# A product-key expert layer on one core: four gathered token tiles, keys in two passes, values in one

## The chip, the core and the metric

The kernel runs on one core of one Trainium2 chip. Its engines work at the same time, each on its own list of instructions, and meet at semaphores: TensorE (PE) multiplies, VectorE (DVE) does elementwise work and top-k, ScalarE (ACT) activations and copies, GpSimd (POOL) here elementwise work and indirect transfers, SyncE (SP) queues the plain transfers. The metric is the device time of one execution in microseconds (us); the figure quoted for a kernel is the median of its runs.

## The reference

One encoder layer over 1024 tokens of width 1024, all in float32. First a mixer (normalise, project, gated linear attention and pooling, project back), which the change does not touch. Then the expert part:

```python
q = (ht @ w_q).reshape(T, 8, 2, 128)                        # 8 retrieval heads, 2 halves
s = einsum('thpd,hpnd->thpn', q, sub_keys)                  # 128 scores per half
vals, idx = top_k(s, 16)                                    # per half
cand = vals[:, :, 0, :, None] + vals[:, :, 1, None, :]      # 16 x 16 sums
top_s, top_pos = top_k(cand.reshape(T, 8, 256), 16)
i1, i2 = the two indices that top_pos picks from idx
experts = i1 * 128 + i2                                     # 128 chosen of 16384 experts per token
gates = softmax(top_s)
a = gelu(h . u[experts]);  y = sum_e gates * a * v[experts]
out = x + gate2 * rmsnorm(y)
```

## The kernel before

Tokens lie in 8 tiles of 128. The 16384 experts lie in 128 blocks of 128. Every float32 product is made of three passes over split operands: an operand is cut into a high and a low part (ACT writes `hi` as a copy in the reduced type, `split_hi`, L78; DVE writes `lo` as the difference, `split_lo`, L83), and PE adds hi·hi, hi·lo and lo·hi (`tile_product`, L93).

**Retrieval** (`retrieval_scores`, L1093). For each of 16 half-heads PE makes a query tile (`tile_product`, 48 matmuls of 512 columns) and then the scores of all 8 token tiles (L1196). In each turn DVE splits both of the next weights first, then takes both scores out of PSUM, and then runs `topk_head` (L1028) for token tile 0 of that head. All scores go to memory (`s_d`), and later each head of a tile comes back as `s_work`.

**Sweep 1** (`expert_sweep_1`, L1264). For each of the 128 expert blocks PE computes the keys' products with all 1024 tokens (48 matmuls of 512 columns), ACT applies gelu (L1415), and the result is stored (`act_d`). Beside it, one head of one token tile after another gets its top-k on DVE. For the first 6 tiles (`DENSE`) the sparse gates become dense matrices: for groups of 8 tokens DVE compares the iota row with the chosen indices in two instructions of 1024 elements (`compare`, L1479), POOL multiplies by the gate in two (L1393), PE makes 8 matmuls of 256 columns (L1555), ACT copies the high part out (L1426) and DVE adds the low part (L1492). The last 2 tiles (`SPARSE`) keep their lists of chosen experts. The order on each engine is written out by hand: a step is two expert blocks, and PE runs product, gates, product, gates, so that a batch of one-hots is compared while PE is in the product before the one after which they are used.

**Sweep 2** (`expert_sweep_2`, L1594). The 6 dense tiles are taken in two rounds of 3, and each round reads all 128 blocks of v. A step is one block: DVE makes the coefficients gate times activation (L1763) and the low parts, ACT the high parts, PE 18 matmuls of 512 columns (L1882) into 3 accumulators. Beside it the 2 sparse tiles are gathered: POOL issues for each of 256 chosen experts an indirect transfer of one activation per token (`pick_acts`, L1666) and one of the v row per token (`fetch_row`, L1674, 512 KB), and DVE adds coefficient times row (`add_row`, L1785). At the end each tile is normalised, scaled and added to x1.

## Time and profile before

| | us |
|---|---|
| runs (3) | 3317.35, 3335.14, 3335.84; median 3335.14 |
| profiled execution, first to last instruction (span) | 3333.3 |
| PE, DVE, ACT, POOL busy in the span | 3133.5, 2255.8, 1016.9, 1005.3 |
| first key matmul of sweep 1 starts | 719.5 |
| first value matmul of sweep 2 starts | 2225.9 |
| last value matmul starts | 3307.1 |
| mean granted clock of PE, whole span | 0.976 |

The page of the profile gives the busy time of each engine; matmuls are pipelined, so their own durations overlap, and what one costs is read from the distance between starts. The span is one execution; what lies around it is the difference to the time of a run, 1.8 us against the median. A timeline merges equal instructions that follow each other and gives their count.

### The profile page before, as it was taken

What the parts mean: (1) busy time and instruction counts of PE and PEld (TensorE: products, weight loads), DVE (VectorE), ACT (ScalarE), POOL (GpSimd) and SP (SyncE); (2) the same over time, 40 slices, a digit from 0 to 9 for tenths busy, and PEclk for the clock granted to TensorE, in tenths of its full rate; (3) what the DMA queues carried; (4) which work ended last, traced back from release to release, by engine and by line L of the source; (5) the groups of instructions that cost most, each with busy time, mean ns of one, the idle gap of its engine ahead of it and who ended that gap; (6) DMA issues with size and microseconds to landing.
All of it is one profiled execution on the core that took longest, in us unless ns stands there. A gap on an engine that the chain in (4) does not pass through costs nothing. (4 is left out here: it accounts for less than half of the span.)

```text
span 3333.3 us, 44756 instructions
## 1 busy us (share of the span) xinstructions
PE 3133.5 (94%) x14706; PEld 2592.3 (78%) x14706; DVE 2255.8 (68%) x3986; ACT 1016.9 (31%) x1301; POOL 1005.3 (30%) x735
## 2 busy tenths in 40 slices
PE   3993799989999999999999999998999998999996
PEld 3881587878888888888888888876888886788885
DVE  6345643567767677675876754436888888888886
ACT  3123442112232232322222221122333334333333
POOL 0000100013222233232332310024555567765541
PEclk9995899999999999999999999999999999999998
DMA  6510122222333324333233332248999999999995
GB/s 235 189 50 8 49 105 93 84 72 113 126 148 139 148 88 151 141 149 137 101 142 145 150 137 106 102 159 299 373 353 361 364 357 332 369 357 364 348 361 186
DMA packets 251520, 640.90 MB, mean 192 GB/s; under 512 B 28864, under 2 KB 134464, under 8 KB 249792
## 3 DMA queue, kind: packets, MB, share of 16 engines
q1 hardware_dynamic: 204528, 498.87, 40.8%
q0 software_dynamic: 46928, 141.20, 11.3%
q8 instruction: 37, 0.61, 0.1%
q14 instruction: 27, 0.22, 0.0%
HBM read 505.76 MB, written 134.22 MB: 192 GB/s over the span
## 5 line engine op out<-in xcount | busy, mean ns | idle before, releaser
L1393 POOL TENSOR_TENSOR onehot<-onehot,slots 128x1024 fp32r<-128x1024 f32 x192 | 368.9, 1943 | 1180.1 <-DVE onehot L1479 1180.1
L93 PE MATMUL acc_u<-a_hi,u_hi 128*128 128x512 f32 x2048 | 633.1, 391 | 2.5 <-PEq L1114 2.5
L93 PE MATMUL acc_u<-a_lo,u_hi 128*128 128x512 f32 x2048 | 632.3, 390 | 0.0
L93 PE MATMUL acc_u<-a_hi,u_lo 128*128 128x512 f32 x2048 | 631.6, 389 | 0.0
L1882 PE MATMUL y_ps<-v_hi,c_hi 128*128 128x512 f32 x1536 | 477.2, 392 | 32.6 <-DVE c_lo L83 26.8
L1882 PE MATMUL y_ps<-v_lo,c_hi 128*128 128x512 f32 x1536 | 475.8, 391 | 0.0
L1882 PE MATMUL y_ps<-v_hi,c_lo 128*128 128x512 f32 x1536 | 474.6, 390 | 0.0
L78 ACT ACTIVATE v_hi<-v_raw 128x1024 fp32r<-128x1024 f32 x256 | 271.6, 1061 | 654.0 <-PE y_ps L1882 544.8
L93 PEld LDWEIGHTS acc_u<-a_lo,u_hi 128*128 128x128 f32 x2048 | 385.0, 188 | 81.0
L93 PEld LDWEIGHTS acc_u<-a_hi,u_lo 128*128 128x128 f32 x2048 | 384.8, 188 | 81.2
L83 DVE TENSOR_TENSOR v_lo<-v_raw,v_hi 128x1024 fp32r<-128x1024 f32 x256 | 316.6, 1237 | 186.4 <-ACT v_hi L78 145.1
L1415 ACT ACTIVATE gelu<-acc_u 128x1024 f32<-128x1024 f32 x128 | 131.5, 1028 | 1013.8 <-PE acc_u L93 1013.8
L93 PEld LDWEIGHTS acc_u<-a_hi,u_hi 128*128 128x128 f32 x2048 | 378.4, 188 | 75.0 <-issue 2.6
L1674 POOL DMA_INDIRECT v_rows<-in_v,eidx x256 | 283.5, 1107 | 358.0 <-DVE y_part L1785 313.4
L1882 PEld LDWEIGHTS y_ps<-v_hi,c_hi 128*128 128x128 f32 x1536 | 288.3, 189 | 99.1 <-DVE v_lo L83 26.0
L1882 PEld LDWEIGHTS y_ps<-v_lo,c_hi 128*128 128x128 f32 x1536 | 289.9, 189 | 60.9
L1882 PEld LDWEIGHTS y_ps<-v_hi,c_lo 128*128 128x128 f32 x1536 | 289.7, 189 | 60.9
L1666 POOL DMA_INDIRECT picked_act<-act_d,aidx x256 | 311.1, 1215 | 77.9 <-issue 77.9
L1785 DVE SCALAR_TENSOR_TENSOR y_part<-v_rows,coef,y_part 128x1024 f32<-128x1024 f32 x256 | 329.2, 1289 | 0.6 <-DMA v_rows<-in_v,eidx 0.5
L83 DVE TENSOR_TENSOR u_lo<-u_raw,u_hi 128x1024 fp32r<-128x1024 f32 x128 | 164.8, 1288 | 207.5 <-ACT u_hi L78 207.5
L1492 DVE TENSOR_TENSOR gate_block<-gate_block,gate_ps 128x1024 f32 (+1 forms) x96 | 116.8, 1216 | 216.0 <-ACT gate_block L1426 216.0
L1479 DVE TENSOR_TENSOR onehot<-consts,slots 128x1024 fp32r<-128x1024 f32 x192 | 239.6, 1290 | 0.9 <-issue 0.9
(228 smaller groups left out, 3414.4 us busy)
## 6 DMA issues: line engine op xcount, KB each, us to landing
v_raw<-in_v SPq DMA_DIRECT2D x256, 512.0 KB
u_raw<-in_u SPq DMA_DIRECT2D x128, 512.0 KB, 4.3
act_d<-gelu SPq DMA_DIRECT2D x128, 512.0 KB, 2.6
gate_d<-gate_block SPq DMA_DIRECT2D x12, 4096.0 KB, 12.1
gt<-gate_d SPq DMA_DIRECT2D x64, 768.0 KB
at<-act_d SPq DMA_DIRECT2D x256, 192.0 KB
w_mod_b<-in_w_mod SPq DMA_DIRECT2D x6, 2560.0 KB, 9.1
w_mod<-in_w_mod SPq DMA_DIRECT2D x9, 1024.0 KB, 16.4
```

Of the source, the lines that this page charges most:

```text
L78: return act.activation(hi, raw, ACT.Copy)
L83: return dve.tensor_tensor(lo, raw, hi.bitcast(F32), ALU.subtract)
L93: done = pe.matmul(acc[:, cols], w, a[:, k, cols], start=first, stop=last)
L1393: last_op = pool.tensor_tensor(onehot_2[u][:, :, part, :], onehot_2[u][:, :, 0, :].bitcast(F32), gate.unsqueeze(2).to_broadcast([P, TOK // ...
L1415: act.activation(gelu[s][:], acc[s][:], ACT.Gelu).then_inc(gelu_done, 1)
L1479: last = dve.tensor_tensor(rows, g.iota.unsqueeze(1).to_broadcast([P, TOK // 2, NKEYS]), chosen.unsqueeze(2).to_broadcast([P, TOK // 2, NK ...
L1492: dve.tensor_tensor(dst, dst, gate_psum(1), ALU.add).then_inc(gate_out, 1)
L1666: pool.indirect_dma_start(out=picked_act[:, e:e + 1], out_offset=None, in_=act_table, in_offset=bass.IndirectOffsetOnAxis(ap=index(g.aidx, ...
L1674: pool.indirect_dma_start(out=rows[e % UNROLL][:], out_offset=None, in_=v_table, in_offset=bass.IndirectOffsetOnAxis(ap=index(g.eidx, e), ...
L1785: dve.scalar_tensor_tensor(sums, rows[k][:], coef[:, k:k + 1], sums, ALU.mult, ALU.add).then_inc(rows_done, 1)
L1882: done = pe.matmul(yps[t][:, cols], c, v[s][:, cols], start=first and k == 0, stop=last and k == 2)
```

## The change

It rewrites everything behind the mixer as one block with every loop written out (no loop instructions). Four token tiles are gathered instead of two and four are dense instead of six. The keys are read twice: steps m = 0 to 127 give the activations of token tiles 0 to 2 (`EARLY`, 384 columns), steps 128 to 255 those of tiles 3 to 7 (`LATE`, two pieces of 320 columns). The values are read once, in steps 256 to 383, for the four dense tiles. The candidate list of a head is cut from 256 to 136 sums (the first row's 16, and 8 of each of the other 15). Top-k of the three early tiles is done together in retrieval, a head at a time; the other five tiles are done in pairs of heads, one or two of 13 stages per step, from step 5 on. The dense gates are made from step 44 on in one batch of 8 tokens every third step, by three short instructions for each token on DVE; POOL has no elementwise work left. The 512 gathered rows begin at step 134, with two in a step, and three in steps 200 to 255. Gate blocks are stored for 16 tokens at a time, and read back in pieces of 512 bytes in place of 1 KB. Rings: 4 raw blocks, 3 split blocks, 7 gathered rows.

```diff
+EARLY = 3
+GATHERED = 4
+LATE = TT - EARLY
+DENSE = TT - GATHERED
 DTOK = DENSE * P
-TILE_STEPS = HEADS + 1
-STEPS = NKEYS // 2
-assert DENSE * TILE_STEPS + HEADS + 2 == STEPS
+HEAD_TILES = EARLY
+STAGES = 4
+RAWS, SPLITS, GELUS, ACTS, ROWS = 4, 3, 3, 4, 7
...
+HEADS_STAGES = ((0, 1, 2), (3, 4, 5), (6, 7, 8, 9), (10, 11, 12))
+STEP_STAGES = ((0, 1), (2,), (3,), (4, 5), (6, 7), (8, 9), (10,), (11,), (12,))
+TOPK_FROM, TOPK_PERIOD = 5, 40
+BATCH = 8
+GTOK = 2 * BATCH
+GROUP = 8
+GATES_FROM, GATES_EVERY = 44, 3
+ROWS_FROM, ROWS_FAST = 134, 200
...
-def topk_head(g, dve, h, topk_done):
...
+def topk_stage(g, dve, stage, scores, tops_out, chosen_out, read_all, done):
...
+    dve.drain()
+    if stage == 0:
+        for c in cs:
+            for p in range(2):
+                dve.max(vals[:, c, p, 0:8], scores[c][p])
+    elif stage == 1:
+        for c in cs:
+            for p in range(2):
+                dve.max_index(idx[:, c, p, 1 - p:9 - p], vals[:, c, p, 0:8], scores[c][p])
+                last = dve.match_replace(rest[:, c, p, :], vals[:, c, p, 0:8], scores[c][p], LOWEST)
...
+    elif stage == 2:
+        for c in cs:
+            for p in range(2):
+                dve.max(vals[:, c, p, 8:16], rest[:, c, p, :])
...
+    elif stage == 3:
+        for c in cs:
+            for p in range(2):
+                dve.max_index(idx[:, c, p, 9 - p:17 - p], vals[:, c, p, 8:16], rest[:, c, p, :])
+        dve.tensor_tensor(cand[:, 0:n, 0:TOPK], vals[:, 0:n, 0, 0:1].to_broadcast([P, n, TOPK]), vals[:, 0:n, 1, :], ALU.add)
+        later = [P, n, TOPK - 1, TOPK // 2]
+        dve.tensor_tensor(cand[:, 0:n, TOPK:].rearrange("p c (a b) -> p c a b", b=TOPK // 2),
+                          vals[:, 0:n, 0, 1:].unsqueeze(3).to_broadcast(later),
+                          vals[:, 0:n, 1, 0:TOPK // 2].unsqueeze(2).to_broadcast(later), ALU.add)
+    elif stage == 4:
+        for c in cs:
+            dve.max(tops[:, c, 0:8], cand[:, c, :])
+    elif stage == 5:
+        for c in cs:
+            dve.max_index(pos[:, c, 0:8], tops[:, c, 0:8], cand[:, c, :])
+            dve.match_replace(spare[:, c, :], tops[:, c, 0:8], cand[:, c, :], LOWEST)
+    elif stage == 6:
+        for c in cs:
+            dve.max(tops[:, c, 8:16], spare[:, c, :])
+    elif stage == 7:
+        for c in cs:
+            dve.max_index(pos[:, c, 8:16], tops[:, c, 8:16], spare[:, c, :])
+        dve.tensor_copy(tops_out, tops[:, 0:n, :])
+    elif stage == 8:
+        dve.tensor_scalar(hilo[:, 0:n, :, 0], pos[:, 0:n, :], 3, None, ALU.logical_shift_right)
+        dve.tensor_scalar(hilo[:, 0:n, :, 1], pos[:, 0:n, :], float(TOPK), 8.0, ALU.is_lt, ALU.mult)
+    elif stage == 9:
+        dve.scalar_tensor_tensor(hilo[:, 0:n, :, 1], hilo[:, 0:n, :, 1], 7, pos[:, 0:n, :], ALU.bitwise_or, ALU.bitwise_and)
+    elif stage == 10:
+        full = [P, n * TOPK * 2, TOPK + 1]
+        dve.tensor_tensor(match, hilo[:, 0:n].rearrange("p c k l -> p (c k l)").unsqueeze(2).to_broadcast(full),
+                          g.iota[:, 0:TOPK + 1].unsqueeze(1).to_broadcast(full), ALU.is_equal)
+    elif stage == 11:
+        full = [P, n, TOPK, 2 * (TOPK + 1)]
+        each = match.rearrange("p (c k l) i -> p c k (l i)", k=TOPK, l=2)
+        dve.tensor_tensor(each, each, idx[:, 0:n].rearrange("p c l i -> p c (l i)").unsqueeze(2).to_broadcast(full), ALU.mult)
+    else:
+        dve.tensor_reduce(chosen_out, match, AX, ALU.add).then_inc(done, 1)
+def rows_by(m):
+    if m < ROWS_FROM:
+        return 0
+    return min(GATHERED * CHOSEN, 2 * (m - ROWS_FROM + 1) + max(0, min(m, 2 * N - 1) - ROWS_FAST + 1))
+def split_expert_hi(g, act, m):
+    act.wait_ge(g.raw_in[m % RAWS], 16 * (m // RAWS + 1))
+    if m >= SPLITS:
+        act.wait_ge(g.tile_done, m - SPLITS + 1)
+    split_hi(act, g.hi[m % SPLITS][:], g.raw[m % RAWS][:]).then_inc(g.hi_ready, 1)
+def expert_product(g, pe, m):
+    pe.wait_ge(g.lo_ready, m + 1)
+    if m >= 2:
+        pe.wait_ge(g.gelu_done, m - 1)
+    else:
+        pe.wait_ge(g.q_out, QTILES - 1 + m)
+    acc, w_hi, w_lo = g.mps[m % 2], g.hi[m % SPLITS], g.lo[m % SPLITS]
+    if m < N:
+        parts = [(acc[:, 0:EARLY * P], slice(0, EARLY * P))]
+    else:
+        wide = LATE * P // 2
+        parts = [(acc[:, half * HALF:half * HALF + wide], slice(EARLY * P + half * wide, EARLY * P + (half + 1) * wide))
+                 for half in range(2)]
+    for k in range(KC):
+        wh, wl = w_hi[:, k * P:(k + 1) * P], w_lo[:, k * P:(k + 1) * P]
+        for w, a, first, last in ((wh, g.a_hi, k == 0, False), (wh, g.a_lo, False, False), (wl, g.a_hi, False, k == KC - 1)):
+            for dst, cols in parts:
+                done = pe.matmul(dst, w, a[:, k, cols], start=first, stop=last)
+    done.then_inc(g.tile_done, 1)
+def retrieval_scalar(g, act):
+    def stage_out(n):
+        act.wait_ge(g.s_done, n + 1)
+        if n >= STAGES:
+            act.wait_ge(g.s_stored[n % STAGES], 16 * (n // STAGES))
+            act.wait_ge(g.heads_read, (n - STAGES) // 2 + 1)
+        act.activation(g.stage[n % STAGES][:], g.sps[n % 2], ACT.Copy).then_inc(g.s_out, 1)
+    for n in range(QTILES):
+        act.wait_ge(g.q_done, n + 1)
+        act.activation(g.q[n % 2][:], g.mps[n % 2][:], ACT.Copy).then_inc(g.q_out, 1)
+        if n + 2 < QTILES:
+            act.wait_ge(g.wq_in[n % 2], 16 * (n // 2 + 2))
+            split_hi(act, g.wq_hi[n % 2][:], g.wq_raw[n % 2][:]).then_inc(g.wq_hi_ready, 1)
+        else:
+            split_expert_hi(g, act, n + 2 - QTILES)
+        if n:
+            stage_out(n - 1)
+    stage_out(QTILES - 1)
+def retrieval_vector(g, dve):
+    def split(n):
+        dve.wait_ge(g.wq_hi_ready, n + 1)
+        split_lo(dve, g.wq_lo[n % 2][:], g.wq_raw[n % 2][:], g.wq_hi[n % 2][:]).then_inc(g.wq_lo_ready, 1)
...
+    for h in range(HEADS - 1):
+        split(2 * h + 2)
+        dve.wait_ge(g.s_out, 2 * h + 2)
+        for stage in range(5):
+            head_stage(g, dve, h, stage)
+        split(2 * h + 3)
+        for stage in range(5, TOPK_STAGES):
...
+            head_stage(g, dve, h, stage)
+    split_expert_lo(g, dve, 1)
+    dve.wait_ge(g.s_out, QTILES)
+def retrieval_tensor(g, pe):
+    def product(n, halves=(0, 1)):
+        pe.wait_ge(g.wq_lo_ready, n + 1)
+        tile_product(pe, g.mps[n % 2], g.wq_hi[n % 2], g.wq_lo[n % 2], g.a_hi, g.a_lo, halves).then_inc(g.q_done, 1)
+    def score(n):
+        pe.wait_ge(g.q_out, n + 1)
+        if n >= 2:
+            pe.wait_ge(g.s_out, n - 1)
+        for t in range(TT):
+            last = pe.matmul(g.sps[n % 2][:, t, :], g.q[n % 2][:, t * P:(t + 1) * P], g.keys[:, n, :], start=True, stop=True)
+        last.then_inc(g.s_done, 1)
+    for n in range(2):
+        product(n, halves=(1,))
...
+    for n in range(2, QTILES):
+        score(n - 2)
+        product(n)
+    score(QTILES - 2)
+    expert_product(g, pe, 0)
+    score(QTILES - 1)
+def sweeps_scalar(g, act):
...
+    for m in range(3 * N):
+        if m >= 2 * N - 1 and m + 1 < 3 * N:
+            split_coefficients(m + 1 - 2 * N)
+        if m + 2 < 3 * N:
+            split_expert_hi(g, act, m + 2)
+        x, batch = gate_turn(m - 1)
+        if x is not None and batch >= 0:
+            gate_evacuation(x * GATE_BATCHES + batch)
...
+        if m < 2 * N:
+            activate(m)
...
+def sweeps_vector(g, dve):
...
+    def onehots(b, u):
...
+        for t in range(BATCH):
+            col = slice(first + t, first + t + 1)
+            high = g.gate_hi[:, col].bitcast(F32)
+            dve.tensor_scalar(g.onehot_1[u][:, t, :], g.iota, g.slots[:, 0, col], None, ALU.is_equal)
+            dve.tensor_scalar(g.onehot_2[u][:, t, 0:NKEYS], g.iota, g.slots[:, 1, col], high, ALU.is_equal, ALU.mult)
+            last = dve.tensor_scalar(g.onehot_2[u][:, t, NKEYS:], g.iota, g.slots[:, 1, col], g.slots[:, 2, col],
+                                     ALU.is_equal, ALU.mult)
+        last.then_inc(g.onehot_ready, 1)
...
+    for m in range(3 * N):
+        if 2 * N - 2 <= m < 3 * N - 2:
+            coefficients(m + 2 - 2 * N)
+        if m + 2 < 3 * N:
+            split_expert_lo(g, dve, m + 2)
+        if 2 * N - 1 <= m < 3 * N - 1:
+            coefficients_lo(m + 1 - 2 * N)
+        first_tiles(m)
+        x, batch = gate_turn(m - 1)
+        if x is not None and batch < 0:
+            take_slots(x)
+        elif x is not None:
+            add_gate_low(x * GATE_BATCHES + batch)
+        topk_steps(m)
+        x, batch = gate_turn(m)
+        if x is not None and batch >= 0:
+            onehots(x * GATE_BATCHES + batch, m // N)
...
+        for e in range(rows_by(m - 1), rows_by(m)):
+            add_row(e)
+            if e % CHOSEN == CHOSEN - 1:
+                sum_gathered(e // CHOSEN)
...
+def sweeps_gpsimd(g, pool):
...
+    turns = GATHERED * CHOSEN // TURN
+    pool.wait_ge(g.chosen_ready, 1)
+    act_complete(N - 1)
+    for s in range(2):
...
+    pick_acts(0)
+    for turn in range(turns):
+        for e in range(turn * TURN, (turn + 1) * TURN):
+            fetch_row(e)
+            if e == turn * TURN and turn + 1 < turns:
+                pick_acts(turn + 1)
+def sweeps_tensor(g, pe):
...
+    def dense_product(n):
+        m = 2 * N + n
+        pe.wait_ge(g.lo_ready, m + 1)
+        pe.wait_ge(g.clo_ready, n + 1)
...
+        for q, t in enumerate(DENSE_ORDER):
...
+            ch, cl = g.c_hi[s][:, t * P:(t + 1) * P], g.c_lo[s][:, t * P:(t + 1) * P]
+            for k, (c, v) in enumerate(((ch, v_hi), (ch, v_lo), (cl, v_hi))):
+                for half in range(2):
+                    cols = slice(half * HALF, (half + 1) * HALF)
+                    done = pe.matmul(g.yps[t][:, cols], c, v[:, cols], start=n == 0 and k == 0, stop=n == N - 1 and k == 2)
+            if n == N - 1:
+                done.then_inc(g.y_summed, 1)
+        if n < N - 1:
+            done.then_inc(g.tile_done, 1)
+    for m in range(2 * N):
+        if m:
+            expert_product(g, pe, m)
+        x, batch = gate_turn(m)
+        if x is not None and batch < 0:
+            transpose_slots(x)
+        elif x is not None:
+            gates(x * GATE_BATCHES + batch, m // N)
+    for n in range(N):
+        dense_product(n)
```

## Rows read from the trace of the kernel before

**Rows 1.** The page, part 1: busy time of each engine, share, instructions.
```profile
PE 3133.5 (94%) x14706; PEld 2592.3 (78%) x14706; DVE 2255.8 (68%) x3986; ACT 1016.9 (31%) x1301; POOL 1005.3 (30%) x735
```
**Rows 2.** Tile views: count, ns min/median/max, first and last start, forms.
```profile
L93 PE MATMUL acc_u<-a_hi,u_hi x2048: 387/389/628, 719.5 to 2217.5; 128*128 128x512 f32 x187
...
L1882 PE MATMUL y_ps<-v_hi,c_lo x1536: 387/389/628, 2227.8 to 3307.1; 128*128 128x512 f32 x192
```
**Rows 3.** Sweep 2: length, busy (count) by engine, clock, DMA share, GB/s.
```profile
2500.00:2600.00 100.00, 100.00 (x443) 82.81 (x442) 83.35 (x102) 36.48 (x50) 56.20 (x51) 1.00 0.98 363
```
**Rows 4.** The chain that ended last: start, length, instruction, count.
```profile
2275.98 488.45 PE y_ps L1882 x2142
```
**Rows 5.** Timeline, sweep 1: start, length, engine, instruction, count [idle before].
```profile
1200.26 1.11 PE L1555 MATMUL gate_ps<-onehot,onehot 128*128 128x256 f32 x8
1200.45 1.03 ACT L1415 ACTIVATE gelu<-acc_u 128x1024 f32<-128x1024 f32 x1 [8.84 <-PE acc_u L93]
1201.21 0.63 PE L93 MATMUL acc_u<-a_hi,u_hi 128*128 128x512 f32 x2
```
**Rows 6.** Timeline of PE in retrieval, around one query tile.
```profile
700.66 1.95 PE L1196 MATMUL s_ps<-keys,q 128*128 x16
...
713.35 3.73 PE L1196 MATMUL s_ps<-keys,q 128*128 128x128 f32 x32
```
**Rows 7.** Timeline of DVE: one head's top-k in sweep 1.
```profile
1207.19 0.48 DVE L1032 MAX8 vals<-s_work 128x8 f32<-128x128 f32 x2
1207.75 0.09 DVE L1035 MATCH_VALUE_LOAD idx<-vals,s_work 128x8 f32 x1
...
1208.28 0.08 DVE L1035 MATCH_VALUE_LOAD idx<-vals,s_work 128x8 f32 x1
...
1210.06 1.43 DVE L1043 TENSOR_TENSOR cand<-vals 128x256 f32<-128x256 f32 x1
...
1214.17 0.17 DVE L1058 TENSOR_SCALAR hilo<-pos 128x16 uint32<-128x16 uint32 x1
1214.25 0.17 DVE L1059 TENSOR_SCALAR hilo<-pos 128x16 uint32<-128x16 uint32 x1
1214.49 0.69 DVE L1062 TENSOR_TENSOR match<-hilo,consts 128x512 f32<-128x512 uint32 x1
```
**Rows 8.** Timeline of DVE: after that head, and early in sweep 1.
```profile
756.29 4.05 DVE L1479 TENSOR_TENSOR onehot<-consts,slots 128x1024 fp32r<-128x1024 f32 x2
...
1216.71 1.21 DVE L1492 TENSOR_TENSOR gate_block<-gate_block,gate_ps 128x1024 f32 x1
1217.84 1.22 DVE L83 TENSOR_TENSOR u_lo<-u_raw,u_hi 128x1024 fp32r<-128x1024 f32 x1
1218.97 2.36 DVE L1479 TENSOR_TENSOR onehot<-consts,slots 128x1024 fp32r<-128x1024 f32 x2
```
**Rows 9.** Groups of DVE instructions: count, busy us, mean ns, idle before.
```profile
L1785 DVE SCALAR_TENSOR_TENSOR y_part<-v_rows,coef,y_part 128x1024 f32<-128x1024 f32 x256 | 329.2, 1289 | 0.6 <-DMA v_rows<-in_v,eidx 0.5
...
L257 DVE TENSOR_SCALAR x<-x,rstd 128x1024 f32<-128x1024 f32 x8 | 5.4, 746 | 0.1
...
L1258 DVE TENSOR_SCALAR aidx<-eidx,token_col 128x128 uint32<-128x128 uint32 x2 | 0.6, 288 | 0.2
```
**Rows 10.** A stretch early in sweep 1, columns as in rows 3.
```profile
740.00:764.00 24.00, 17.60 (x74) 14.66 (x73) 22.96 (x54) 6.13 (x6) 13.34 (x7) 0.79 0.21 71
```
**Rows 11.** Timeline of PE in that stretch: gate matmuls after a wait.
```profile
749.85 2.08 PE L1555 MATMUL gate_ps<-onehot,onehot 128*128 128x256 f32 x8 [6.40 <-DVE gate_block L1492]
```
**Rows 12.** Timeline of POOL in sweep 2: indirect transfers, issued without waiting.
```profile
2504.78 1.67 POOL L1666 DMA_INDIRECT picked_act<-act_d,aidx  x1 [0.30 <-issue]
...
2516.68 0.94 POOL L1674 DMA_INDIRECT v_rows<-in_v,eidx  x1 [0.30 <-issue]
...
2549.32 0.94 POOL L1674 DMA_INDIRECT v_rows<-in_v,eidx  x1 [0.30 <-issue]
...
2553.41 0.93 POOL L1674 DMA_INDIRECT v_rows<-in_v,eidx  x1 [0.30 <-issue]
```

1212 lines of the change are left out of this document (473 added, 739 removed).

## The prediction, before the result was known

> **What bounds the kernel now.** The page's first part says PE is busy 94% of the span [rows 1], so I read PE first: the tile views give the ends of the stages, sweep 1 from 719.5 and the last value matmul at 3307.1 [rows 2], that is 2587.6 us for both sweeps and 26 us behind them. Next the distance between starts. A run of 2142 matmuls of 512 columns takes 488.45 us, 0.228 each [rows 4]; 8 matmuls of 256 columns take 1201.21 - 1200.26 = 0.95, 0.119 each [rows 5]. Between the two I interpolate 0.146 for 320 columns and 0.1735 for 384. The old work at these prices is 128 x 48 x 0.228 = 1401, plus 96 gate batches x 0.95 = 91, plus 256 x 18 x 0.228 = 1051: 2543 of the 2588. So PE's rate is the bound and all else together costs 45 us. In sweep 2 the transfers are near their own limit, busy 0.98 at 363 GB/s [rows 3]. DVE is busy 68% [rows 1] and hides, since its work stands a step ahead of PE.
>
> **PE's own work after.** An early key step is 24 x 0.1735 = 4.16 us, a late one 48 x 0.146 = 7.01, a dense value step 24 x 0.228 = 5.47. Times 128: 533, 897 and 700. Gates: 64 batches x 0.95 = 61. Sum 2191, which is **-397** against the 2588. The whole gain is here: 1536 fewer value matmuls, paid with only 29 us for the second reading of the keys.
>
> **Retrieval: a new wait.** Before, DVE splits both next weights before it turns to the scores. After, `split(2h+3)` stands behind stages 0 to 4 of head h, and head h begins only when both its scores are out; PE makes score 2h+1 directly ahead of product 2h+3, which needs that split. So from the end of product 2h+2: ACT copies the query, splits, copies the scores, 3 x 1.03 = 3.1 [rows 5]; then DVE's stages for 3 tiles. MAX8 costs 0.24, an index search with its replacement 1208.28 - 1207.75 = 0.53 [rows 7], half of that for a search alone. 6 x 0.24 + 6 x 0.53 + (6 x 0.24 + 0.1) + (6 x 0.26 + candidates 1.8) + 3 x 0.25 + 5 drains x 0.07 = 10.6 (candidates: 360 elements at the 1.2 to 1.43 per 256 of [rows 7]). Then the split, 1.13 [rows 8]. Together 14.9, where PE would start after the score, 12.69 [rows 6] - 10.94 = 1.75. That is 13.1 a head, 7 heads: 92. The second half (stages 5 to 12: 9.8 by the same rows, with three instructions of 1632 elements scaled from 0.69 per 512) ends before product 2h+3 does. After such a gap PE also restarts at the half clock: one wait of 6.4 us left 8 gate matmuls at 2.08 instead of 1.11 [rows 5, 11] and a granted clock of 0.79 over 24 us [rows 10]; 74 matmuls in 17.6 busy us where 15.1 would do, 2.5 lost. 7 x 2.5 = 17. **+109**, with cover gone completely: it's in order on PE.
>
> **Gates: DVE can't be ahead of PE.** The high split of block m+2 waits for product m-1 (3 split buffers), DVE begins step m with that block's low split, and then come low-gate addition, top-k, and last the one-hots that PE waits for right behind product m. What is queued behind the wait on PE is product m+1, on ACT the gate copy and the next gelu. From the end of product m-1: gelu of 384 columns 0.4, split 1.03 [rows 5], low split 1.13 [rows 8], a drain 0.07, top-k 1.3 (in the gate steps mostly stages 2, 3, 5 to 9, 11, 12 of two heads), one-hots. These are 24 instructions of 128 elements per batch, a form the trace doesn't show. Nearest: one with a pointer scalar and 128 elements takes 288 ns [rows 9], and followers start about 0.085 before the end of the one ahead (0.17 against 1214.25 - 1214.17 = 0.08 [rows 7]; 1.22 against 1.13 [rows 8]); two thirds of them have a second pointer. I take 0.21, a batch 5.1. Ends: 0.14 (between the 0.08 for 16 elements and 746 ns for 1024 [rows 7, 9]), 3.4 a batch; 0.26 if they run at one element a cycle, 6.3. So the one-hots are there 9.05 us after the end of product m-1 and PE at 4.16: 4.9 a batch. Early: 26 batches, 127. Half-clock restarts: 20 (26 x 2.5 = 65 at most, as the waits are shorter than 6.4; zero at least). The last head's top-k (20 us in steps 0 to 3 beside 4.16 a step, two steps of slack): 6. **+153**.
>
> The VectorE page of the Trainium skill (VectorE: DVE Perf Modes, Mode 2×_2P) says a float32 instruction with a single source in SBUF takes two elements a cycle and one with two sources takes one. The 746 ns for 1024 elements beside 1.22 for a difference [rows 8, 9] agree; by it the upper end falls away.
>
> **Late keys.** Gelu of 640 columns is 0.7, so the one-hots come at 2.95 + 5.1 + top-k 2.0 (1.3 in the fifth tile) against 7.01: 3.0 and 2.3. 22 batches: 58. The 2 rows a step cost DVE 1.2 each [rows 9] and fit. From step 200 to 255 three rows are taken in each step, 168 rows. POOL pays per row one pick, (2516.68 - 2504.78)/8 = 1.49, and one fetch, (2553.41 - 2549.32)/3 = 1.36 [rows 12]: 2.85, so 8.55 a step; ring and DVE are in order, and PE follows two steps later. 56 x 8.55 = 479 against 408 of PE: 71. Lower end 1.24 + 1.24, the shortest with their 0.30 [rows 12]: 9. POOL's issues beside short DVE instructions: a comparison pair took 4.05 early in sweep 1, while POOL multiplied, and 2.36 in [rows 8] without it, so the two engines do hold each other up. For 15 batches I take 2 us each of 5.1: 30, between zero and 77. **+159**.
>
> **Dense values.** A step moves 512 KB of v, 256 of activations, 256 of gates and two rows of 512: 2.10 MB. At 363 GB/s over 0.98 [rows 3] that is 5.66, and the 512-byte pieces are not better; POOL's two rows want 5.7. I take 5.8 in 106 steps: +35 against 5.47 (ends 0 and +67, at 6.1). DVE has 0.6 + 1.13 + 0.6 + 2.4 + 0.1 = 4.85 and fits. Hand-over between the passes: **+40** together. Stores of gates and activations, the x1 loads on SP and the 3.7 us of finishing a gathered tile lie beside PE and I cost them at nothing; they'd show as up to 4 us for each of 4 tiles.
>
> **Tail.** Before, 26 us from the last matmul, with a sparse tile's finish in the way. After, four tiles end 1.4 us apart in PE and DVE needs 2.7 each: 12. **-14**.
>
> Sum: -397 + 109 + 153 + 159 + 40 - 14 = +50, so the profiled 3333.3 becomes 3383; the median lies 2 above its span: **3385 us, slower by 1.5%**.
>
> **Rivals.** (A) *The short one-hots are cheap.* At 0.14 a piece and without half-clock restarts: 48 batches x 1.7 = 82 and 20 less, 3283: faster. For it: 0.08 for a 16-element instruction. Against: 288 ns. It ends on the other side of the old time from 4.1 us a batch down, 3.4 being its end. (B) *POOL and the transfers keep up*: 62 + 30 + 35 less, 3258, faster; for it the shortest issues, against it that every eight picks in [rows 12] average 1.49. (C) *POOL is locked out.* If the DVE's short instructions keep it out for the whole batch, 15 x 5.1 = 77 in place of 30, and with every early wait restarting at the half clock, 45: 3477.
>
> The SBUF page (SBUF — State Buffer, Who interferes with whom) states this as a rule for the Trainium skill's single-source DVE modes: GpSimd can't write its transfer descriptors while such an instruction runs. No run here shows it for transfers. By that rule case C's 47 us would be the price.
>
> (D) *The wait in retrieval isn't there*, because I misread the order: 109 less, 3276.
>
> **Numbers.** Main case 0.50, its own range 3310 to 3460 (one-hots by 0.02 a piece is 23 us, POOL 30, transfers 30, restarts 20). A 0.17, B 0.12, C 0.15, D 0.04, the rest 0.02. The range of 8 in 10 reaches into A and B below and C above: 3240 to 3490; all low ends at once would be 3133, all high ends 3515. A measurement of this kernel can tell about 1% from no change, 3302 to 3368. Faster: over half of A, most of B and D, a little of the main case, 0.26. Within 1%: the rest of A and B and a fifth of the main case, 0.23. Slower 0.51.
>
> **What the changed profile would show.** PE idle some 13 us ahead of each odd query product, released by the DVE split; the first key matmul of step 1 about 110 later. One-hot instructions starting 0.21 apart, PE idle 4.9 before each early gate batch and 2 to 3 before late ones. Key steps from 200 on at 8.5 us, DVE waiting for row transfers. Dense steps at 5.8, transfers busy near 1. It'd be wrong at once if PE is busy over 95% between first key and last value matmul.

## The result: 9.8% slower, outside the range

The changed kernel takes **3658.2 us** (median of 4 runs, 3651.1 to 3669.8), the kernel before 3334.5 beside it (3317.4 to 3335.8): ratio **1.098**, interval 1.095 to 1.101. Forecast were 3385 and at most 3490. The direction was right, the size wrong by 273 us.

The profiled execution spans 3657.6 us. The page's first part, which answers to [rows 1] (engine, busy us, share of the span, instructions), has a PE that is no longer the bound by itself:

```profile
PE 3003.9 (82%) x15980; PEld 2705.5 (74%) x15980; DVE 2400.1 (66%) x5118; ACT 940.1 (26%) x1262; POOL 1313.0 (36%) x1033
```

The tile view of the key and value products (first and last start) gives the ends of the stages, as [rows 2] did:

```profile
L1308 PE MATMUL mix<-a_hi,hi x3072: 302/309/633, 814.2 to 2820.8; 128*128 128x320 f32 x128, 128*128 128x384 f32 x64
...
L1774 PE MATMUL mix<-hi,free_hi_r x680: 387/389/628, 2829.8 to 3645.8; 128*128 128x512 f32 x170
```

Against the prediction's own terms, put together by stage (us; the end of the early key steps, 1583, is the start of the gelu of the last of them):

| stage | predicted | measured | miss |
|---|---|---|---|
| up to the first key product | 828 | 814 | -14 |
| 128 early key steps | 711 | 768 | +57 |
| 128 late key steps | 1092 | 1239 | +147 |
| 128 value steps | 740 | 824 | +84 |
| tail | 12 | 12 | 0 |

Four stretches of it by engine (length, then busy us of PE, its weight loads, DVE, ACT, POOL, granted clock, transfer share, GB/s; compare [rows 3, 10]): early key steps with gates, late ones at two rows a step, late ones at three, value steps:

```profile
1000.00:1584.00 584.00, 438.62 (x2286) 430.31 (x2285) 394.02 (x1252) 159.86 (x208) 0.00 (x0) 0.87 0.41 134
1640.00:2254.00 614.00, 537.64 (x3422) 526.45 (x3421) 470.53 (x1134) 137.82 (x162) 324.00 (x262) 0.94 0.67 227
2254.00:2822.00 568.00, 471.62 (x2818) 448.75 (x2817) 394.52 (x663) 115.62 (x138) 387.91 (x333) 0.87 0.75 262
2845.00:3499.00 654.00, 571.23 (x2350) 462.99 (x2349) 475.88 (x518) 161.55 (x199) 535.88 (x388) 0.94 0.89 318
```

PE is full in none of them, and neither are the transfers. GpSimd is, in the last one: 535.88 us busy and 0.30 between any two of 388 transfers make 652 of the 654 us, though the page counts only the first as busy. What ended PE's idle time (what waited, for what, total us, times, longest):

```profile
PE sps_all L1756 <- DVE onehot L1567: 145.4, 26, 7.5
PE mix L1308 <- issue: 87.0, 120, 2.4
PE mix L107 <- DVE wq_lo L97: 82.2, 8, 11.6
PE sps_all L1756 <- DVE free_hi_r L1567: 73.8, 26, 6.2
PE sps_all L1774 <- DVE free_hi_r L97: 49.4, 12, 5.9
...
PE sps_all L1756 <- issue: 27.6, 15, 5.0
```

The one-hots and the retrieval wait are the two that were forecast. The second line was in no theory: "issue" is time in which PE waited for nothing that the profile shows, 87 us of it in the middle of key products. Sweep 1 before had none. The last line, ahead of gate matmuls, is mostly something else. Its long waits end right behind the last one-hot of their batch, as here (PE, then DVE):

```profile
1750.80 1.44 PE L1756 MATMUL sps_all<-free_hi_r 128*128 128x256 f32 x5 [4.98 <-issue]
```
```profile
1750.41 0.33 DVE L1567 TENSOR_SCALAR free_hi_r<-consts,slots 128x128 fp32r<-128x128 f32 x1
```

So about 24 of the 27.6 us are the forecast wait for one-hots under another name, and some 90 us in all are not explained. They look like this, PE first (start, length, instruction, count, idle before) and then GpSimd at the same time:

```profile
1602.91 0.46 PE L1308 MATMUL mix<-a_lo,hi 128*128 128x320 f32 x2
1603.20 0.65 PE L1308 MATMUL mix<-a_hi,lo 128*128 128x320 f32 x2
1604.25 0.31 PE L1308 MATMUL mix<-a_hi,hi 128*128 128x320 f32 x1 [0.39 <-issue]
1604.97 0.31 PE L1308 MATMUL mix<-a_hi,hi 128*128 128x320 f32 x1 [0.41 <-issue]
1605.68 0.41 PE L1308 MATMUL mix<-a_lo,hi 128*128 128x320 f32 x1 [0.40 <-issue]
1607.08 0.43 PE L1308 MATMUL mix<-a_lo,hi 128*128 128x320 f32 x1 [0.98 <-issue]
1608.47 0.43 PE L1308 MATMUL mix<-a_hi,lo 128*128 128x320 f32 x1 [0.97 <-issue]
```
```profile
1587.19 1.16 POOL L1714 DMA_INDIRECT picked_act<-act_early,aidx  x1 [1172.49 <-DMA act_early<-gelu]
...
1607.72 0.94 POOL L1714 DMA_INDIRECT picked_act<-act_early,aidx  x1 [0.30 <-issue]
1608.97 0.94 POOL L1721 DMA_INDIRECT rows<-in_v,eidx  x1 [0.30 <-issue]
...
1615.19 0.94 POOL L1721 DMA_INDIRECT rows<-in_v,eidx  x1 [0.30 <-issue]
```

Two matmuls together had taken 0.29 from start to start; now each starts by itself, 0.70 or 1.40 after the one ahead. It begins some 16 us after GpSimd started to issue and ends at 1619.7, 3.5 us after GpSimd paused. I call PE **held** here. "Held" times below are the issue waits less those that end right behind a one-hot.

### The profile page after: what moved, and what is told of

The parts are those of the page before. It is cut to its first block, busy times and chain, and to the rows that moved or that the text cites. A ratio compares the mean times of both kernels' runs of the same rounds, so it can differ in the third digit from the quotient of the medians.

```text
span 3657.6 us, 43230 instructions
## 1 busy us (share of the span) xinstructions
PE 3003.9 (82%) x15980; PEld 2705.5 (74%) x15980; DVE 2400.1 (66%) x5118; ACT 940.1 (26%) x1262; POOL 1313.0 (36%) x1033
## 3 DMA queue, kind: packets, MB, share of 16 engines
q0 software_dynamic: 90112, 268.76, 21.0%
q8 instruction: 123, 2.02, 0.2%
## 4 chain that ended last, share of the span: by engine, by line
PE 42%; DVE 15%; POOL 15%; issue 9%; ACT 2%; DMA 1%; DVEq 1%; another core or an unknown queue 0%; SPq 0%; ACTq 0%; POOLq 0%
PE mix L1308 30%; POOL picked_act L1714 8%; POOL rows L1721 7%; PE mix L107 5%; PE sps_all L1756 3%; DVE lo L97 2%; PE sps_all L1774 2%; PE mix L1774 2%; ACT hi L92 2%; DVE free_hi_r L1567 2%; DVE onehot L1567 1%; DVE onehot L1566 1%; DVE free_hi_r L1566 1%; DVE onehot L1565 1%; DVE free_hi_r L1565 1%
## 5 line engine op out<-in xcount | busy, mean ns | idle before, releaser
L1714 POOL DMA_INDIRECT picked_act<-act_early,aidx x384 | 465.6, 1213 | 1289.2 <-DMA act_early<-gelu 1172.5
L1308 PE MATMUL mix<-a_hi,hi 128*128 128x320 f32 (+1 forms) x3072 | 853.3, 332 | 29.5 <-issue 24.4
L1308 PE MATMUL mix<-a_hi,lo 128*128 128x320 f32 (+1 forms) x3072 | 847.7, 330 | 34.2 <-issue 33.8
L1308 PE MATMUL mix<-a_lo,hi 128*128 128x320 f32 (+1 forms) x3072 | 850.2, 330 | 28.9 <-issue 28.8
L97 DVE TENSOR_TENSOR lo<-raw,hi 128x1024 fp32r<-128x1024 f32 x384 | 469.2, 1222 | 572.9 <-ACT hi L92 477.9
L1721 POOL DMA_INDIRECT rows<-in_v,eidx x512 | 643.0, 1256 | 473.8 <-DVE ys L1626 279.2
L1626 DVE SCALAR_TENSOR_TENSOR ys<-rows,coef,ys 128x1024 f32<-128x1024 f32 x504 | 627.6, 1281 | 168.4 <-DMA rows<-in_v,eidx 151.7
L1308 PEld LDWEIGHTS mix<-a_hi,hi 128*128 128x128 f32 x3072 | 568.1, 200 | 40.5 <-issue 35.1
L1308 PEld LDWEIGHTS mix<-a_hi,lo 128*128 128x128 f32 x3072 | 565.6, 198 | 41.8 <-issue 41.8
L1308 PEld LDWEIGHTS mix<-a_lo,hi 128*128 128x128 f32 x3072 | 568.1, 199 | 34.6 <-issue 34.6
```

The lines of the kernel that those rows point to most:

```text
L97: return dve.tensor_tensor(lo, raw, hi.bitcast(F32), ALU.subtract)
L1308: done = pe.matmul(dst, w, a[:, k, cols], start=first, stop=last)
L1626: dve.scalar_tensor_tensor(sums, row, coef, sums, ALU.mult, ALU.add).then_inc(g.rows_done, 1)
L1714: pool.indirect_dma_start(out=g.picked_act[:, e:e + 1], out_offset=None, in_=act_tables[e // (EARLY * CHOSEN)], in_offset=bass.IndirectOff ...
L1721: pool.indirect_dma_start(out=g.rows[e % ROWS][:], out_offset=None, in_=v_table, in_offset=bass.IndirectOffsetOnAxis(ap=index(g.eidx, e), ...
```

## Experiments

All edits are on the changed kernel. Stage times are from each run's own profile, "late" and "value" between the gelus of products 127 and 255 and the last matmul. 

### The waits that were forecast

**gates_next**: gate matmuls one product later.
```
-        gates(x * GATE_BATCHES + batch, m // N)        # x, batch = gate_turn(m)
+        gates(x * GATE_BATCHES + batch, (m - 1) // N)  # x, batch = gate_turn(m - 1)
```
(the copy, the low addition and the store follow with `gate_turn(m - 2)`).

> The gate matmuls of a batch stand one product later on PE (and their copy, low addition and store one step later); the one-hots are made where they were. Theory O (PE idles because the one-hots are always last on DVE): PE has a product of 4.16 or 7.0 us to cover the 5.6 us of one-hots, so the idle time before gate matmuls (145 us early, 74 late) and the half-clock restarts behind it (some 50) go: early key steps 769 to about 600, late ones 1237 to about 1160, total 3658 to 3400-3440. Rival S (the split ring: the low split two steps on only comes behind the one-hots, so the wait merely moves to the next product): less than 60 us gained. Nothing changes in retrieval (814 to the first key product) or in the value stage (824).

3427.2 us, **231 gained**: early 759 to 613, late 1239 to 1154, value unchanged at 824 ("early" is from the gelu of product 0 to that of product 127). Theory O holds, rival S falls. The wait for the one-hots early fell from 145 to 40.

**split_first**: both retrieval splits ahead of the stages of a head.
```
     split(2 * h + 2)
+    split(2 * h + 3)
     dve.wait_ge(g.s_out, 2 * h + 2)
-    for stage in range(5): head_stage(g, dve, h, stage)
-    split(2 * h + 3)
-    for stage in range(5, TOPK_STAGES):
+    for stage in range(TOPK_STAGES):
```

> DVE splits both next query weights of retrieval before it turns to the scores, as in the kernel before; nothing else differs. Theory W (the 82 us in 7 longer waits of PE for that split, with a restart at the half clock behind each, are the whole of what retrieval lost): first key product 90 to 105 us earlier, total 3555 to 3570. Rival V (the work of DVE in a head, 26 us, is then the bound by itself): gain under 50.

3651.6 us, 7 gained: the key stage began 25 earlier, and 20 were given back in the stages behind. W falls. The trace shows why: DVE now makes both splits behind the whole head, and the wait has only moved to the even product. PE, and DVE at the next head:

```profile
647.90 1.22 PE L107 MATMUL mix<-a_hi,wq_hi 128*128 128x512 f32 x2 [9.22 <-DVE wq_lo L97]
```
```profile
646.64 2.35 DVE L97 TENSOR_TENSOR wq_lo<-wq_raw,wq_hi 128x1024 fp32r<-128x1024 f32 x2
664.86 1.26 DVE L1044 MAX8 vals<-stage 128x8 f32<-128x128 f32 x6 [15.87 <-ACT stage L1341]
```

DVE is idle for 16 us in this head (107.6 in 7 such waits), so DVE's load is not the bound (rival V falls too): the head, the split, the product, the score and the next head form a ring.

**next_and_first**: the two together.

> Gate matmuls one product later and both splits of retrieval first, together. If the two lie in different stages and add up: 3427 less the gain of the split alone (90 to 105), 3322 to 3340, level with the kernel before. If something is shared (the key stage begins earlier but waits for a load or the top-k): over 3360.

3357.7 us: 70 less than with gates_next, between the two expectations. Only 29 of it is the earlier first gelu (800 for 829); the late stage took 1118 for 1154 and the value stage 816 for 824. PE was held less (74 us for 129), which the edit wasn't meant to change. So gains of some ten us behind retrieval can't be put down to an edit alone: in split_first the late stage grew by 33.

**next_and_spread**: gates_next, and the splits spread over the head.
```
+    split(2); split(3)
     for h in range(HEADS - 1):
-        split(2 * h + 2)
         ... stages 0 to 4
-        split(2 * h + 3)
+        if h < HEADS - 2: split(2 * h + 4)
         ... stages 5 to 12
+        if h < HEADS - 2: split(2 * h + 5)
```

> Gate matmuls one product later, and in retrieval the split for product 2h+4 stands after stage 4 of head h and the one for 2h+5 behind stage 12 (with both splits first, 25 us came back of 82). Theory R (retrieval is a ring: DVE's head of 24 us, split, product, score, next head, so the place of the split within the head decides): no wait for the query weights' low halves over 2 us, first key product about 95 us earlier than with the kernel as changed, total 3427 - 95 = 3320 to 3345. Rival V (DVE with 24 us of top-k and two splits a head against 25.4 us of PE is itself the bound): half of it, 3370 to 3390.

3305.1 us (7 runs, 3290 to 3325); ratio to before 0.990, interval 0.988 to 0.992. The wait for wq_lo is gone from the list and the first gelu comes at 731 in place of 824 (829 in gates_next), which is when it came in the kernel before. Theory R holds, though the total is 15 below its range: the ring was the whole of retrieval's loss.

### What the gather costs, and by what

**no_gather, rows_only, picks_only**: GpSimd issues nothing, or only the rows, or only the picks. In each, DVE's multiply-adds stay, with constants for what isn't fetched.
```
-    dve.wait_ge(g.rows_in[e % ROWS], ...)               # no_gather, picks_only
-    pool.indirect_dma_start(out=g.rows[e % ROWS][:], ...)   # picks_only
-    pick_acts(turn + 1)                                 # rows_only
-    turns = GATHERED * CHOSEN // TURN
+    turns = 0                                           # no_gather
```

> Leaves out the gather's transfers: GpSimd issues no picks and no rows; DVE does the same 512 multiply-adds from a constant tile, so its work is unchanged. It measures all that the gather's transfers cost. If the excess of the late key stage (1237 us where PE's own work is 897 + 24) is from the gather, by theory P (GpSimd's issuing holds up PE's and ACT's issue) or T (bytes moved): late stage 1030 to 1060, the one-hot waits (74) staying; value stage 824 to 715-740; total 3658 to 3350-3390. Rival D (DVE's load of one-hots, multiply-adds and splits is the bound in the late stage, whatever is gathered): late stage stays above 1180, total above 3550.

> Leaves out the 512 picks of activations (4 bytes a partition, 0.2% of the gather's bytes, half of GpSimd's instructions); the rows are fetched, DVE's work is the same with constant activations. Theory P (what costs is GpSimd issuing back to back): with half the instructions it is idle half the time, the 115 us of issue waits of PE nearly vanish, late stage about 1080 to 1120, value stage about 740, total 3420 to 3470. Theory T (bytes and DMA engines): nothing to speak of changes, total over 3620. Between them (rows and picks cost alike): 3500 to 3560.

> Leaves out the 512 row fetches (all but 0.2% of the gather's bytes); the 512 picks of 4 bytes a partition are issued in their bursts of 8, and DVE's multiply-adds take a constant row. Leaving all of the gather's transfers out gave 3375 us, leaving out the picks alone 3389, the kernel as changed 3658. Theory N (it's the number of instructions that GpSimd issues, which only with picks and rows together exceeds what fits in a step): 3380 to 3420, as with rows alone. Theory K (the kind: a pick, with its 4-byte packets, holds PE and ACT up as such): 3580 to 3650. Additive (a pick costs half a microsecond wherever): 3640.

| kernel | time | late | value | PE held |
|---|---|---|---|---|
| as changed | 3658.2 | 1239 | 824 | 90 |
| no_gather | 3375.0 | 1080 | 697 | none |
| rows_only | 3388.9 | 1083 | 712 | none |
| picks_only | 3396.7 | 1101 | 697 | 5 |

The gather's transfers cost 283 us, 159 in the late key stage and 127 in the value stage; rows alone, with nearly all the bytes, cost 14, picks alone 22. So each kind alone costs little, and both together cost much. For the rows alone every theory had expected more (3420 at least), and no_gather's late stage is 20 above its forecast. The rows' bytes are no bound: with the rows alone the value steps take 5.56 us at more bandwidth than [rows 3] had (500 us of it):

```profile
2700.00:3200.00 500.00, 499.39 (x2203) 413.21 (x2202) 447.15 (x486) 148.93 (x188) 271.62 (x184) 1.00 1.03 385
```

**rows_halved**: no picks, each row in two transfers.
```
+    for c in (0, HALF):
+        pool.indirect_dma_start(out=g.rows[e % ROWS][:, c:c + HALF], in_=v_halves, ...)
```

> Leaves out the picks and fetches each row in two indirect transfers of 512 elements instead of one of 1024 (of another row of v, so the values are not the reference's): the bytes of the rows alone, but again 1024 instructions on GpSimd, none of them a pick. Theory N (number of instructions): 3600 to 3660, PE's issue waits come back (over 60 us). Theory K (the picks' kind): as with rows alone, 3380 to 3420. A middle value of 3480 to 3540 would say that both count.

3636.6 us, late 1240, value 808, PE held for 69. With no pick but again 1024 instructions nearly the whole loss is back: the **number** of GpSimd's instructions decides. How much of it is their queue and how much is PE being held, this doesn't separate.

**even**: one pick behind each row in place of 8 at a time.
```
-            if e == turn * TURN and turn + 1 < turns:
-                pick_acts(turn + 1)
+            if turn + 1 < turns:
+                pick_acts(turn + 1, [e % TURN])
```

> The picks are no longer issued 8 at a time but one behind each row; same transfers, same number, same work. Theory P1 (PE and ACT are held up only when GpSimd issues without a pause for longer than some ten us): at two rows a step the runs are 5 us, so the issue waits go in steps 134 to 199 and the late stage falls by 80 to 150 us; total 3510 to 3580. Theory P2 (each issue costs PE or ACT the same wherever it stands): no change, 3640 to 3670. Theory T (bytes): no change either. Rival R: rows are issued only every 2.5 us, which is late for DVE in the three-row steps and the value stage: slower by 10 to 40.

3639.8 us, 18 gained; P1's 80 to 150 was wrong. By steps it is less simple: steps 134 to 199 took 585 in place of 601 (578 with no gather) and had next to no held time between 1624 and 2251 (under 1 us; 11 us as changed), where GpSimd's runs without a pause have at most 12 instructions (14 as changed). But at three rows GpSimd has more to issue than fits, its runs get as long as 84, and the steps from 200 took 591 in place of 568 (448 with no gather). There was little to gain where the runs could be cut.

### Who holds PE

**unwaited**: the transfers are issued, nobody waits for them.
```
-    dve.wait_ge(g.rows_in[e % ROWS], 16 * (e // ROWS + 1))
+    sums, row = g.ys[e % 2][:], g.gate_rows[:, 0, :]     # and iota for picked_act
-    pool.wait_ge(g.rows_done, e - ROWS + 1)
+    pool.wait_ge(g.rows_in[e % ROWS], 16 * (e // ROWS))
```

> All 1024 indirect transfers are issued as in the kernel as changed, but nobody waits for them: DVE's multiply-adds take a constant row and constant activations, and GpSimd only waits for the landing of the row seven before. So GpSimd issues nearly without a pause from the 128th key product on, for about 1024 x 1.3 to 1.5 = 1300 to 1500 us. Theory F (freeze: when GpSimd has issued for some 15 us without a pause, PE's and ACT's issue is held up, whoever waits for the rows): PE's issue waits well over the 115 us of the kernel as changed, several hundred us in the late key stage, total above 3650. Theory Q (queueing alone: GpSimd brings the rows late and DVE, in order, waits for them with the splits behind): no issue waits, 3375 to 3420, as with no transfers at all.

**4348.7 us**: late 2056, value 697. Theory Q falls. PE in the held state, and ACT's gelu behind it:

```profile
1889.65 0.43 PE L1308 MATMUL mix<-a_hi,hi 128*128 128x320 f32 x1 [2.37 <-issue]
1892.45 0.43 PE L1308 MATMUL mix<-a_hi,hi 128*128 128x320 f32 x1 [2.37 <-issue]
1895.25 0.43 PE L1308 MATMUL mix<-a_lo,hi 128*128 128x320 f32 x1 [2.37 <-issue]
```
```profile
1851.87 0.70 ACT L1503 ACTIVATE gelu<-mix 128x640 f32<-128x640 f32 x1 [132.75 <-issue]
```

One matmul in 2.80 us. A key product in steady state, 48 weight loads and 48 matmuls, takes 134.4 us, and in that time GpSimd issues exactly 96 transfers (112 in 156.8 us where 8 gate matmuls come on top): **one instruction of PE for one transfer of GpSimd**. In the kernel as changed the hold was mostly milder: a matmul and its weight load in 0.70 or 1.40 us, beside one transfer in 1.25. The SBUF page of the Trainium skill (SBUF — State Buffer, Who interferes with whom) says, of the ports into SBUF, that PE and ACT never wait on anyone. PE was held here; that it was at such a port isn't shown.

**keys24, dense48, plain**, all on unwaited: 24 matmuls of 512 columns in a late key product; 48 of 256 in a value step; plain transfers on the same queue.
```
+    parts = [(acc[:, 0:HALF], slice(EARLY * P, EARLY * P + HALF))]   # keys24
-    for half in range(2):       # columns of 512
+    for quarter in range(4):    # columns of 256                     # dense48
-    pool.indirect_dma_start(out=g.rows[e % ROWS][:], ...)
+    pool.dma_start(g.rows[e % ROWS][:], g.i["v"][e % N])             # plain
```

> On the same kernel the late key products take one matmul of 512 columns where they took two of 320 (24 a product; the products of one of five tiles, and which columns, are left out: the activations are not the reference's). Theory I: key steps are no longer held up; late key stage 128 x 5.5 + 24 + the waits for one-hots at a shorter step (4 to 5 us for 38 batches) = 880 to 950, total 3150 to 3250. Theory K: still 2.80 us a matmul while GpSimd issues, 24 of them 67 us a step: late key stage above 1600, total above 3900.

> On the kernel in which nobody waits for the gather (4349 us; key stage held up, value stage 697 us though GpSimd issued 263 transfers in its first 463 us), each value step takes 48 matmuls of 256 columns in place of 24 of 512. Theory I (PE is sensitive where its instructions come as thick as in the key steps, one matmul per 0.12 to 0.15 us): the value stage is held up while GpSimd issues, 2.8 us a matmul, value stage 1100 to 1200, total 4750 to 4850. Theory K (sensitive is something else of the key stage: its tiles, its PSUM banks, the store of the activations, the early table): only the narrower matmuls show, 48 x 0.119 = 5.7 a step, value stage 730 to 750, total 4380 to 4400.

> On the same kernel GpSimd issues 1024 plain transfers of the same shapes (a fixed row of v, a fixed column of the early activations) in place of the indirect ones. Theory S (every transfer that GpSimd prepares holds PE up): key stage held up as before, total above 4000. Theory X (only indirect ones do): 3375 to 3420, as with no transfers.

keys24: 4200.1, late 1906, still held, at 48 transfers a product: one for one again. dense48: 4540 (the profiled run; the other took 4714), value stage 886; next to untouched for 256 us and then held too, from 3900 until GpSimd was done, at 2.80 a matmul. So neither theory is right: thin instruction streams can be held, and the value stage can be. With its 512-column matmuls it was not: as changed, GpSimd's 388 transfers without a pause held PE nowhere in it. plain: 3464.2, late 1080, no issue wait; theory S falls. PE isn't held while the transfers run at 399 GB/s:

```profile
1780.00:1820.00 40.00, 35.15 (x215) 34.89 (x215) 30.48 (x68) 8.14 (x10) 23.16 (x44) 0.88 1.03 399
```

That clears bytes and packets (90112 packets and 268.76 MB on GpSimd's queue, as in unwaited) of holding PE. They aren't free, though: the total is 44 above theory X, since the value stage took 787. DVE waited there 93 us, in 4 waits, for activations to land, and the transfers' share was 1.02 for its first 239 us. GpSimd was also busy less (0.53 us a transfer, with pauses), so the run doesn't prove that unbroken plain issuing is harmless.

**dense_idle, spaced, unwaited_again**: multiply-adds of 32 columns in the value stage; three small memsets ahead of each transfer; unwaited unchanged.

> On the kernel in which nobody waits for the gather (4349 us), DVE's multiply-adds in the value stage are cut from 1024 to 32 columns, so that DVE is idle there for 2 us more in each step; PE's work is as before. Theory R (PE is held up where GpSimd's transfers follow at their shortest distance, 1.25 us; in the value stage DVE's work stretches them to 1.76): GpSimd speeds up to 1.3 to 1.4 a transfer and PE is held in the value stage, value stage 900 to 1050, total 4550 to 4700. Theory E (what PE executes decides, or whether it has to wait): value stage 697, total 4350, whatever GpSimd's distance.

> On the same kernel GpSimd sets a small spare tile to zero three times ahead of each transfer, and waits for each, so that transfers follow about 1.8 to 2.2 us apart, still without an idle moment on GpSimd. Theory R: PE isn't held up, late key stage 1080 to 1130, total under 3450 (GpSimd's 1024 transfers may outlast the value stage, and then the end is later by that). Theory E or F (GpSimd's being busy all the time decides): one PE instruction per transfer as before, now 2 us each: late key stage over 2100.

> The same kernel as unwaited (4349 us in two rounds), run again in another session. If being held up goes with the kernel (its instruction streams and their exact timing), all rounds are again held: 4330 to 4370, late key stage 2050. If it goes with the session or the chip, it isn't held: 3390 to 3410, late key stage about 1090, as with dense_idle. If it falls at random, rounds of both kinds show side by side.

3404.3, 4051.7 and **3399.1** us. None of the three was held at all (late 1094, 1083 and 1094; spaced is long because PE waits once, for 656 us, in the value stage: SyncE queues nothing more until the last transfer has landed). The last is the kernel that had taken 4348.7. Here are the same 40 us of it in the session of unwaited and in that of unwaited_again:

```profile
1780.00:1820.00 40.00, 6.17 (x15) 4.04 (x14) 0.00 (x0) 0.00 (x0) 30.17 (x33) 0.50 0.61 212
```
```profile
1780.00:1820.00 40.00, 33.20 (x201) 32.94 (x201) 33.02 (x75) 7.14 (x9) 32.08 (x27) 0.87 0.82 302
```

So being held goes with the session. In the session of the result and the four after it, PE was held in every kernel with over 1000 indirect transfers to issue, and the median of the kernel before was 3334 to 3345; in the last two sessions it wasn't held, and that median was 3321 and 3317. The chip alone doesn't decide it: the record has chip number 5 for the session of keys24 and dense48, where PE was held, and for that of unwaited_again, where it wasn't. dense_idle and spaced ran in such a session and say nothing about what triggers it. What they do show is GpSimd's price beside DVE. The same 380 us of the value stage, dense_idle first, then unwaited_again:

```profile
2700.00:3080.00 380.00, 373.97 (x1639) 309.46 (x1640) 198.05 (x369) 113.23 (x144) 295.37 (x278) 0.99 1.03 389
```
```profile
2700.00:3080.00 380.00, 375.09 (x1646) 310.48 (x1647) 340.70 (x370) 113.95 (x144) 314.16 (x217) 0.99 0.95 346
```

278 transfers against 217: 1.37 us each where DVE is half idle, 1.75 beside its full multiply-adds. A plain transfer kept its 0.53 (23.16 us for 44 in the stretch above) with DVE busy 30.48 of 40. By the same page and section of the Trainium skill an instruction of DVE with two SBUF inputs contends with a GpSimd instruction that reads SBUF, and not with one that only writes it. The trace agrees as far as it goes: only the transfers that take a list of indices from SBUF grew.

### A version that beats both

**uniform**: next_and_spread, even picks, and 2.5 rows a late key step from step 131 and 1.6 a value step. **paced**: besides, GpSimd waits for product m-3 ahead of each row of step m.
```
-    return min(GATHERED * CHOSEN, 2 * (m - ROWS_FROM + 1) + max(0, min(m, 2 * N - 1) - ROWS_FAST + 1))
+    late = min(m, 2 * N - 1) - ROWS_FROM + 1             # ROWS_FROM = 131
+    return min(GATHERED * CHOSEN, (5 * late + 1) // 2 + max(0, 8 * (m - 2 * N + 1) + 4) // 5)
+    pool.wait_ge(g.tile_done, steps[e] - 2)              # paced
```

> As next_and_spread, and the gather is spread evenly: one pick behind each row, 2.5 rows a late key step from step 131 and 1.6 a value step (before: 2 a step, and 3 from step 200 to 255), to end at step 379. GpSimd's load is then at most about 0.9 in each stage instead of over 1 in two of them. Theory N with a load limit: the issue waits of PE under 40 us, late key stage about 1020 to 1060, value stage 720 to 750, total 3150 to 3230. Rival (a load of 0.9 with interleaved picks is still without a pause, so PE and ACT are still held up): 3280 and more.

> The evenly spread gather (3168 us), with one more wait: GpSimd issues the rows of step m, and the picks between them, only when product m-3 is done, so it has a pause in each step instead of runs of 16 to 224 instructions; everything is computed. Theory F (only unbroken runs of over about 12 instructions hold PE up): issue waits of PE under 20 us (102 before), late key stage 1120 to about 1030, total 3060 to 3110. Rival L (the load of 0.8 to 0.9 holds PE up whatever its pauses): 3150 to 3190. Rival B (GpSimd falls behind, since it can't work ahead any more): over 3190.

uniform: **3168.2 us** (3147 and 3189), late 1121, value 708. paced: **3165.7 us** (5 runs, 3146 to 3174), ratio to before **0.948**, interval 0.945 to 0.950. The value stage got back all but 11 us of its 127. PE was held for 98 and then 76 us: the 40 expected of uniform and F's 20 were wrong, and rival L's range was met. GpSimd was often behind, so that the added wait made few pauses (runs of up to 86 transfers stayed in the key stage), and it brought nothing measurable; what full pauses would do isn't settled by it.

## Why the prediction was wrong

The bound was PE plus waits, as forecast. What failed are three terms of the sum: the late keys (+159, measured 306 with a count of batches too low by 16), the restarts behind early gates (20, measured about 49) and the value steps (+40, measured 124). Even all its high ends together, 3515, stay below the measured 3658, so no rival had the time.

**PE's own work: right.** Steps of 4.2 and 7.0 us stand between the gates, and the value steps take 697/128 = 5.45 without the gather, so the hand-over between the passes, priced within the +40, cost nothing.

**Retrieval: right in size, wrong in structure.** The waits were 11.6 us (predicted 13.1), the stage 95 longer (109). But I took the late split for the cause and DVE's order for a detail; moving it to the front gave 25 back. The term that held was the ring.

**Early gates: right mechanism, size 57 short.** The row of one-hots in the trace after (start, length):

```profile
1587.79 0.28 DVE L1565 TENSOR_SCALAR free_hi_r<-consts,slots 128x128 fp32r<-128x128 f32 x1
1587.99 0.39 DVE L1566 TENSOR_SCALAR free_hi_r<-consts,slots,gate_hi 128x128 fp32r<-128x128 f32 x1
1588.24 0.34 DVE L1567 TENSOR_SCALAR free_hi_r<-consts,slots 128x128 fp32r<-128x128 f32 x1
```

Starts are 0.20 apart after one pointer scalar and 0.25 after two: 5.6 a batch where I took 5.1, a wait of 5.6 for 4.9, +18. The rest is the step "half-clock restarts: 20". A batch behind such a wait:

```profile
1324.10 2.07 PE L1756 MATMUL sps_all<-onehot,onehot 128*128 128x256 f32 x8 [5.68 <-DVE onehot L1567]
```

That is the 2.08 of [rows 11], and the following product began at the half clock too: its first matmuls start 0.32 apart, its later ones 0.17.

```profile
1326.29 0.52 PE L1308 MATMUL mix<-a_lo,hi 128*128 128x384 f32 x1
1326.61 0.52 PE L1308 MATMUL mix<-a_hi,lo 128*128 128x384 f32 x1
...
1331.03 0.33 PE L1308 MATMUL mix<-a_hi,hi 128*128 128x384 f32 x1
1331.20 0.33 PE L1308 MATMUL mix<-a_lo,hi 128*128 128x384 f32 x1
```

The gelus of such a step are 12.6 apart: 4.16 of product, 0.95 of gates, 5.6 of wait, and 1.9 that only the restart leaves, 26 x 1.9 = 49. I had the 2.5 of a 6.4 us wait in hand and took 0.8 "as the waits are shorter". The 18 and the 29 make 47 of the 57; the other 10 aren't taken apart here.

**Late keys: 147 short, in two parts.** no_gather separates them. Without any transfer the stage took 1080 where my terms without POOL's give 897 + 36 + 58 = 991: **I multiplied by 22 batches, and there are 38** (64 in all, as I had it myself under PE's own work). The wait was 99.5 in place of 58 (2.6 a batch, as forecast). The other 47 are what is left for restarts, which I gave only to the early ones. The gather then cost 159 where "71 + 30" stood. Its mechanism failed: I priced POOL as a queue that DVE waits for (3 rows a step, 8.55 us). POOL's own price was near that: in the stretch from 2254 to 2822 its 387.91 us busy and 333 pauses of 0.30 make 8.7 for each of 56 steps. But the steps took 10.1. DVE waited only 23 us for rows there and 103 for ACT's high split, POOL itself 81 for DVE to be done with a row, and PE was held for some 63 (issue waits of L1308). With the half clock behind them and each of these feeding the next I can't split the 159 further.

**Value steps: 84 short, the wrong term.** I compared transfers (5.66, taken as 5.8) with POOL (5.7), both too near the step to matter. Transfers gave 15 (rows_only). POOL's price was the one: 388 transfers in the 654 us above are 1.685 each, 3.37 a row with its pick in place of 2.85, 6.74 for two. The 106 steps up to the last row took 6.5 each (688 us from the gelu of product 255 to the last transfer, with some rows issued ahead), and DVE waited 129 us for rows. Why a row cost more than in [rows 12] is only in part shown. DVE's multiply-adds do lengthen a transfer (278 against 217 above), but its busy share alone doesn't tell the distance: at [rows 12] it was 9.77 of 11.90 us, here 475.88 of 654.

**Rivals.** A, B and D are excluded: one-hots at 5.6, POOL behind, the wait in retrieval there. C had the size nearest (3477) with the parties reversed: GpSimd was never shut out for a batch; PE was held while GpSimd issued. Its dearer restarts were nearer than mine (45 more, measured some 29 more).

**Open.** What puts a session in the state in which PE is held, what starts it (16 us or 256 us into a run), and how long this kernel takes in a session without it; that was not tried, so the share of being held in the 9.8% isn't known. Nor is its mechanism: the profile shows only that PE waited for no other engine's work while GpSimd and the transfers went on. Late loads of instructions (123 packets, 2.02 MB in the page of the profile) are a rival that no run excludes, though PE's even pace, 2.80 us a matmul, speaks against it. The page NOTIFIC — the notification-queue block of the Trainium skill (section 7.1, Overflow: three behaviours, one of which stalls the engine) describes a queue of records that, in one of its three modes, stalls the engine that produces them when it is full. No run here shows whether that is what happened.

## What to carry to other kernels

Count GpSimd's indirect transfers as instructions, at the distance that they have beside the DVE work of that very stage (here 1.7, not 1.25), and keep their sum clearly under the step; bytes came second here. Spread them over all steps. A consumer that stands right behind its producer's last work should stand one product later; and before a wait is moved, draw the ring that it belongs to. Give every count in a sum the same source.
